# Scaling expert rows by the router weight on their way out of PSUM, and adding them to the residual in memory by an accumulating scatter

## The reference, cut to what matters

```
h = h + mixer_block(rms_norm(h, norm1[l]), ...)
h = h + hier_moe(rms_norm(h, norm2[l]), ...)
return rms_norm(h, norm_f)

# in hier_moe
gates = jnp.sum(jax.nn.one_hot(expert_id, N_EXPERTS, dtype=f32) * top_w[..., None], axis=1)
for e in range(N_EXPERTS):
    h = jax.nn.silu(xt @ w_g[e]) * (xt @ w_u[e])
    out = out + gates[:, e:e + 1] * (h @ w_d[e]).astype(f32)
```

## Time and profile before

| | |
|---|---|
| three runs | 993.78, 997.96, 1000.33 us (median 997.96) |
| the profiled execution | 997.03 us, of which the span that the profile covers is 995.2 us |
| busy over the span | PE 90%, DVE 66%, ACT 49%, POOL 9% |
| memory traffic of the span | 168.30 MB read, 13.07 MB written |
| experts (700 to 940 us) | DMA engines busy throughout |
| mean granted TensorE clock | 0.954 of full speed |

### The profile page before, as it was taken

One profiled execution on the slowest core, in us unless ns is written; L12 is line 12 of the kernel. 1 busy time (PEld: TensorE's weight loads), 2 busy tenths in 40 slices (PEclk: granted clock), 3 DMA queues, 4 the chain that ended last, 5 costly groups with the idle time before them and its releaser, 6 DMA issues.

```text
span 995.2 us, 14556 instructions
## 1 busy us (share of the span) xinstructions
PE 895.0 (90%) x5884; PEld 511.0 (51%) x5884; DVE 657.2 (66%) x864; ACT 490.3 (49%) x684; POOL 91.7 (9%) x90
## 2 busy tenths in 40 slices
PE   5999999999999998999999989518999999989960
PEld 4434784857656564444444489514545444444420
DVE  3677769533886776443444245454899998988926
ACT  5434373324445444323232325614888878778812
POOL 7000000003000000000000000010121122322100
PEclk9999999999999999999999989758999999999985
DMA  8712414437310115933432260283999999999706
GB/s 206 165 31 63 109 35 114 128 86 149 86 32 17 38 38 193 305 94 96 117 100 83 77 213 2 90 314 131 316 394 388 371 365 376 371 369 366 293 24 251
DMA packets 147247, 174.02 MB, mean 175 GB/s; under 512 B 14391, under 2 KB 99695, under 8 KB 147174
## 3 DMA queue, kind: packets, MB, share of 16 engines
q1 hardware_dynamic: 139760, 158.56, 47.7%
q0 software_dynamic: 7136, 13.89, 5.0%
q10 hardware_dynamic: 278, 0.56, 0.2%
HBM read 168.30 MB, written 13.07 MB: 182 GB/s over the span
## 4 chain that ended last, share of the span: by engine, by line
PE 74%; DMA 11%; DVE 10%; ACT 3%; issue 1%; ACTq 0%; POOLq 0%; DVEq 0%; SPq 0%
PE bank L915 20%; PE bank L916 19%; PE bank L917 19%; DMA arena<-in_moe_wu 6%; DMA arena<-in_moe_wg 4%; PE bank L1127 3%; DVE arena L1645 3%; PE bank L1146 3%; ACT arena L800 1%; PE bank L1021 1%; PE bank L1136 1%; PE bank L1284 1%; DMA arena<-x_rows,token_of 1%; PE bank L1218 1%; PE bank L1006 1%
## 5 line engine op out<-in xcount | busy, mean ns | idle before, releaser
L915 PE MATMUL bank<-arena 128*128 128x512 f16 (+1 forms) x1568 | 465.2, 317 | 13.1 <-DVE arena L1392 4.6
L916 PE MATMUL bank<-arena 128*128 128x512 f16 (+1 forms) x1568 | 464.5, 316 | 0.0
L917 PE MATMUL bank<-arena 128*128 128x512 f16 (+1 forms) x1568 | 464.1, 316 | 0.0
L1645 DVE SCALAR_TENSOR_TENSOR arena<-arena 128x2048 f16<-128x2048 f32 x96 | 216.9, 2288 | 50.2 <-ACT arena L800 50.1
L915 PEld LDWEIGHTS bank<-arena 128*128 128x128 f16 x1568 | 155.1, 99 | 141.5 <-issue 33.8
L917 PEld LDWEIGHTS bank<-arena 128*128 128x128 f16 x1568 | 154.9, 99 | 111.3 <-issue 3.2
L916 PEld LDWEIGHTS bank<-arena 128*128 128x128 f16 x1568 | 154.7, 99 | 99.9 <-issue 3.0
L800 ACT ACTIVATE arena<-arena 128x2048 f16<-128x2048 f32 x96 | 181.5, 1909 | 40.1 <-PE bank L1234 12.5
L567 ACT ACTIVATE arena<-arena 128x1024 f16<-128x1024 f32 (+1 forms) x92 | 92.5, 1007 | 101.3 <-PE bank L917 73.5
L1392 DVE SCALAR_TENSOR_TENSOR arena<-arena 128x1024 f16<-128x1024 f32 (+1 forms) x91 | 103.5, 1163 | 11.4 <-ACT arena L567 9.8
L621 ACT ACTIVATE arena<-bank 128x512 f32<-128x512 f32 x35 | 20.8, 595 | 90.8 <-PE bank L917 90.7
(11 more groups left out here) (257 smaller groups left out, 735.9 us busy)
## 6 DMA issues: line engine op xcount, KB each, us to landing
arena<-in_moe_wg SPq DMA_DIRECT2D x32, 1024.0 KB, 16.4
arena<-in_moe_wu SPq DMA_DIRECT2D x32, 1024.0 KB, 16.3
arena<-in_moe_wd SPq DMA_DIRECT2D x32, 1024.0 KB, 15.3
arena<-in_w_gate SPq DMA_DIRECT2D x32, 512.0 KB, 4.1
arena<-in_w_in SPq DMA_DIRECT2D x31, 512.0 KB, 4.3
arena<-in_w_branch SPq DMA_DIRECT2D x32, 192.0 KB, 3.5
arena<-in_w_out SPq DMA_DIRECT2D x8, 512.0 KB, 5.2
arena<-y_rows SPq DMA_DIRECT2D x4, 1024.0 KB, 8.3
```

The source lines that it names most:

```text
L915: pe.matmul(outb, lhs[0], rhs[0], start=first, stop=False, skip_group_check=True)
L916: pe.matmul(outb, lhs[0], rhs[1], start=False, stop=False, skip_group_check=True)
L917: return pe.matmul(outb, lhs[1], rhs[0], start=False, stop=last_, skip_group_check=True)
L1645: tell("split_done", stt(w_lo[c % NW], stage[c % NS], WSCALE, w_hi[c % NW], ALU.mult, ALU.subtract))
```

## The change

Each expert's rows are scaled by the router weight when ACT copies them from PSUM: the scale is now a column `slotw[:, e]`, one number for each slot. The scatter writes them to `h_rows`, which holds one row for each token, with the operation add: the DMA reads the row in memory, adds, and writes it back. `h_rows` (the first 512 rows of the old `y_rows`) is filled with the residual by eight stores behind the `h_done` of each column block. Scatter e now waits for scatter e-1 to have landed, since two experts may add to the same row (before, it waited for e-2). At the end SP loads one row for each token (0.5 MiB for each tile) and DVE adds nothing; in the place of its two operations stands one on a single column, which only passes the signal on. For `slotw`, DVE puts the weights as two float16 halves into `told`, which has a fourth column, and adds them up again after `token_full`. The second-choice mask, `row_of` and the wait of SP for the last split go. After the `Tanh` of the last expert ACT issues a `Sqrt` on one column.

```diff
@@ sync
+            for m in range(KD):
+                sp_.wait_ge(S("h_done"), m + 1)
+                sp_.dma_start(h_rows.rearrange("(t p) n -> p t n", p=P)[:, :, m * P:(m + 1) * P], hres[:, :, m * P:(m + 1) * P]
+                              ).then_inc(S("h_stored"), 16)
             for t in range(NT):
                 sp_.wait_ge(S("x2_ready"), t + 1)
@@
-                sp_.wait_ge(S("split_done"), len(STEPS))
                 for t in range(NT):
-                    sp_.dma_start(yg[t], y_rows.rearrange("(j t p) n -> t p j n", j=2, p=P)[t]
-                                  ).then_inc(S(f"tokens_in{t}"), 16)
+                    sp_.dma_start(hres[:, t, :], h_rows[t * P:(t + 1) * P, :]).then_inc(S(f"tokens_in{t}"), 16)
@@ gpsimd
-                        if e >= 2:
-                            pool.wait_ge(S(f"y_stored{e % 2}"), 16 * (e // 2))
-                        pool.indirect_dma_start(out=y_rows, out_offset=bass.IndirectOffsetOnAxis(ap=row_of[:, e:e + 1], axis=0),
-                                                in_=yout[e % 2], in_offset=None, bounds_check=2 * T - 1, oob_is_err=False
-                                                ).then_inc(S(f"y_stored{e % 2}"), 16)
+                        if e >= 1:
+                            pool.wait_ge(S(f"y_stored{(e - 1) % 2}"), 16 * ((e - 1) // 2 + 1))
+                        else:
+                            pool.wait_ge(S("h_stored"), 16 * KD)
+                        pool.indirect_dma_start(out=h_rows, out_offset=bass.IndirectOffsetOnAxis(ap=token_of[:, e:e + 1], axis=0),
+                                                in_=yout[e % 2], in_offset=None, bounds_check=T - 1, oob_is_err=False,
+                                                compute_op=ALU.add).then_inc(S(f"y_stored{e % 2}"), 16)
@@ scalar
                         act.activation(sgr[e % 2], ps[2 * (e % 2)][:, :], ACT.Tanh, scale=0.5 / WSCALE).then_inc(S("sgr_ready"), 1)
+                        if e == NE - 1:
+                            link(act.activation(stat[:, 2, 0:1], ones[:, 0:1], ACT.Sqrt))
@@
+                        if e == 0:
+                            act.wait_ge(S("slotw_ready"), 1)
                         for j in range(2):
                             act.activation(yout[e % 2][:, 512 * j:512 * (j + 1)], ps[4 + j][:, :], ACT.Copy,
-                                           scale=1.0 / (WSCALE * HSCALE)).then_inc(S("y_out"), 1)
+                                           scale=slotw[:, e:e + 1]).then_inc(S("y_out"), 1)
@@ vector
-            link(dve.tensor_copy(told[:, :, 1, :], selj[:, 1, :, :]))
-            link(dve.memset(told[:, :, 2, :], 1.0))
+            link(dve.memset(told[:, :, 1, :], 1.0))
+            link(tt(selj[:, 0, :, :], selj[:, 0, :, :], w1.to_broadcast([P, NT, NE]), ALU.mult))
+            link(tt(selj[:, 1, :, :], selj[:, 1, :, :], w2.to_broadcast([P, NT, NE]), ALU.mult))
+            link(tt(gates[:, :, :], selj[:, 0, :, :], selj[:, 1, :, :], ALU.add))
+            link(ts(gates[:, :, :], gates[:, :, :], W16, None, ALU.mult))
+            link(dve.tensor_copy(told[:, :, 2, :], gates[:, :, :]))
+            link(tt(told[:, :, 3, :], gates[:, :, :], told[:, :, 2, :], ALU.subtract))
             dve.wait_ge(S("rank_full"), 1)
@@
+            link(dve.tensor_copy(slotv[:, 2, :], got[:, 2, :]))
+            sig("token_read", tt(slotv[:, 2, :], slotv[:, 2, :], got[:, 3, :], ALU.add))
+            sig("slotw_ready", ts(slotw[:, :], slotv[:, 2, :], 1.0 / (WSCALE * HSCALE * W16), None, ALU.mult))
@@
                 def add_rows(t):
                     dve.wait_ge(S(f"tokens_in{t}"), 32)
-                    link(stt(hres[:, t, :], yg[t][:, 0, :], wsel[:, 0, t:t + 1], hres[:, t, :], ALU.mult, ALU.add))
-                    sig("moe_done", stt(hres[:, t, :], yg[t][:, 1, :], wsel[:, 1, t:t + 1], hres[:, t, :], ALU.mult, ALU.add))
+                    sig("moe_done", ts(total[:, 1:2], total[:, 0:1], 1.0, None, ALU.mult))
```

More of the change, by code:

```diff
@@ L46 @@
 HSCALE = 1.0 / 16
+W16 = 1024.0
 AHEAD = 4
@@ L283, in build @@
                 .rearrange("p (k c) -> p k c", c=P) for j in range(2)] for i in range(2)]
-        yg = [view(STAGE[t], 2, D) for t in range(NT)]
         nf = arena[:, 8192:8192 + D]
@@ L330, in build @@
         wsel = sb("wsel", [P, 2, NT])
-        told = ctx.enter_context(nc.sbuf_tensor("told", [P, NT, 3, NE], F16))
+        told = ctx.enter_context(nc.sbuf_tensor("told", [P, NT, 4, NE], F16))
         slotv = sb("slotv", [P, 3, NE])
-        row_of = ctx.enter_context(nc.sbuf_tensor("row_of", [P, NE], U32))
+        slotw = sb("slotw", [P, NE])
         token_of = ctx.enter_context(nc.sbuf_tensor("token_of", [P, NE], U32))
@@ L341, in build @@
         rt_bank = (ps[6], ps[7], ps[2], ps[3])
-        scratch, x2_rows, y_rows = d["bias_scratch"], d["x2_rows"], d["y_rows"]
+        scratch, x2_rows, h_rows = d["bias_scratch"], d["x2_rows"], d["y_rows"][0:T, :]
         MIXW = 20 + 1 + 1
@@ L1233, in _ @@
                 for t in range(NT):
-                    last = pe.matmul(ps[7][:, 3 * e:3 * e + 3], onehot[:, t, :].rearrange("p (c e) -> p e c", e=NE)[:, e, :], told[:, t, :, e],
+                    last = pe.matmul(ps[7][:, 4 * e:4 * e + 4], onehot[:, t, :].rearrange("p (c e) -> p e c", e=NE)[:, e, :], told[:, t, :, e],
                                      start=(t == 0), stop=(t == NT - 1))
@@ L1730, in _ @@
             dve.wait_ge(S("token_full"), 1)
-            got = ps[7][:, 0:3 * NE].rearrange("p (e a) -> p a e", a=3)
-            link(ts(slotv[:, 0, :], got[:, 2, :], -float(NOWHERE), float(NOWHERE), ALU.mult, ALU.add))
+            got = ps[7][:, 0:4 * NE].rearrange("p (e a) -> p a e", a=4)
+            link(ts(slotv[:, 0, :], got[:, 1, :], -float(NOWHERE), float(NOWHERE), ALU.mult, ALU.add))
             link(tt(slotv[:, 1, :], slotv[:, 0, :], got[:, 0, :], ALU.add))
             link(dve.tensor_copy(token_of[:, :], slotv[:, 1, :]))
-            sig("token_read", stt(slotv[:, 2, :], got[:, 1, :], float(T), slotv[:, 1, :], ALU.mult, ALU.add))
-            link(dve.tensor_copy(row_of[:, :], slotv[:, 2, :]))
+            link(dve.tensor_copy(slotv[:, 2, :], got[:, 2, :]))
+            sig("token_read", tt(slotv[:, 2, :], slotv[:, 2, :], got[:, 3, :], ALU.add))
+            sig("slotw_ready", ts(slotw[:, :], slotv[:, 2, :], 1.0 / (WSCALE * HSCALE * W16), None, ALU.mult))
             sig("dense_known", ts(total[:, 1:2], total[:, 0:1], 1.0, None, ALU.mult))
```

## The result

The changed kernel takes 1008.5 us (median of four runs, 1005.94 to 1009.02) against 995.87 us for the kernel before (four runs, 993.55 to 1000.33): a ratio of 1.0117, 95% interval 1.0089 to 1.0145. It is 1.2% slower, a small loss, but the interval leaves no room for equal times. The forecast was 1009, which is 11.8 us above the profiled execution of before; the medians lie 12.6 apart. The profiled execution took 1008.41 us with a span of 1006.6, which is 11.4 above the span before.

What follows compares the result with a forecast made beforehand. The prediction took the DMA engines to bound the expert stage. Its terms, -8.2 + 15.6 + 1.3 + 1.6 + 1.5 = +11.8 us on the profiled 997.03, gave 1008.8, stated as 1009, with a range of 991 to 1016 (0.8).

Steps and rivals of the forecast that it cites:

- The bound: Expert stage, about 700 to 914 us: bound by the DMA engines, so DMA work added there comes out in full.
- The add among the loads: Twelve scatters ahead of the last wait for a load: each add costs a second transfer, 12 x 1.3 = +15.6 us.
- The last scatter: Scatter alone on the chain after the experts: longer by the same price of an add, +1.3 us.
- The end: Final normalisation and stores: smaller loads and no DVE sums, then a circle of 1.9 us per tile; -8.2 us.
- The early root: ACT's Sqrt in the last expert: table load and root stand ahead of the last split, PE waits; +1.6 us.
- Routing: Between masks and first gather: eight DVE operations in place of three, one more before `dense_known`, all on the path; +1.5 us.
- At nothing: Stores of `h`, scatter e's wait for e-1, ACT's scale from a column: claimed to cost nothing.
- A free second read: Rival on scatters: the add's second read runs beside the first or loads don't feel it; 992 us, chance 0.17.
- Felt as a mean: Rival on scatters: less loaded engines take over, 0.65 us per add; 1000 us, chance 0.13.
- Dearer: Rival on scatters: each row read, added and written in turn, three times the plain transfer; 1026 us, chance 0.15.

Runs made afterwards that it cites:

- run 3: The kernel before, with its first twelve scatters issued a second time to a buffer nothing reads, no adding: 1010.61 us, ratio 1.0139.
- run 7: The kernel before with only the table of slot numbers changed, so an expert's slots are dealt out over the partitions: 987.97 us, ratio 0.9909.
- run 1: The changed kernel with all 16 scatters as plain writes in place of adds: 989.59 us, ratio to before 0.9939.
- run 2: The changed kernel with adds in the last four scatters alone, plain writes in the first twelve: 993.91 us, ratio to before 0.9970.
- run 4: The changed kernel with its Sqrt moved out of the experts to the head of the end, ahead of the first square: 1005.43 us, ratio to before 1.0091.
- run 5: The changed kernel without the Sqrt after the last expert's Tanh: 1006.66 us, ratio to before 1.0108.
- run 8: The kernel before with slots dealt out over the partitions and a Sqrt on one column at the head of the end: 986.86 us, ratio 0.9893.

## Why the prediction was right

**The bound.** "The expert stage is bound by the DMA engines": run 3 adds nothing but DMA work there and is 14.2 us slower, run 7 only spreads the same transfers over more DMA engines and is 9 us faster.

**The add among the loads** was put at 12 x 1.3 = 15.6 us. The trace has 13.9, runs 1 and 2 leave 14.6 for it. The step from 18.37 to 19.67 us per expert is the forecast's 19.7. That a row of an add takes twice the engine time is shown by the 98 against 197 GB/s of the scatter alone, and that the price is that of a second transfer by run 3. The count of twelve was read from the trace of before. In the changed kernel the last load that the chain waits for lands at 960.31, behind fourteen scatters (the last of them issued at 956.72), and 14 x 1.3 = 18.2 would be further off. Why the total stays below is not settled, and neither is what the low clock inside the experts (last section) adds to it.
The Trainium skill's rule (Collectives: The Full Stack, The bandwidth ceiling), that in a collective a reduce step runs at half the rate of a copy for its second source read, agrees in size: its 1.93 stands against 2.0 here (98 against 197 GB/s). Which of the two reads holds the engine no run shows.

**The last scatter** was sized too low: +1.3 forecast, +2.7 measured (5.92 against 3.19; 5.98 in run 2, 3.19 in run 1). The doubling of the rows' time is there, but alone in the queues the add also has gaps between rows, 3.5 us for 64 rows. Dealt over all engines it still takes 4.81, where the plain one takes 2.70.

**The end** was put at -8.2 and is -7.6. The two table loads stood where the program's order had them, one in idle time (981.35), one between square and root (994.43).

**The early root**: forecast +1.6, measured 7.0 against 5.4 us, and taken out again in run 4. The drain of 1.38 us that the Trainium skill gives for a switch (ScalarE: Activation LUTs, What ACT_TABLE_LOAD costs) isn't in these rows: the load at 960.33 is followed by the root at 961.62.

**Routing**: forecast +1.5, measured 1.2 up to the ranks and 0.2 behind. I took it as wholly on the path; 0.8 us came back before the third expert's transposes.

**At nothing**: right for the stores of `h` and the new wait (run 1 holds both, and an expert takes 18.3 us there). None of the sixteen scatters was held by the new wait: POOL sat idle before each of them for ACT's copy (121.1 us in all), and an add landed within 11.4 us of its issue. Wrong for ACT's scale from a column: the two copies to `yout` take 1.27 us in place of 1.09.

**The rivals.** A free second read (992) falls with run 1, which shows 18.9 us for the adds. Felt as a mean (1000): the distance of the gathers in run 3 speaks against it. Dearer (1026) holds in part only for the scatter that is alone. The mechanism held, but that the forecast came within 1 us is partly luck, because misses cancel. Against the forecast the trace has 1.7 less for the adds among the loads, 1.4 more for the last scatter, 0.6 more at the end, and 0.9 less for routing. It also has 0.2 for ACT's slower copy, 1.5 us of the mixer and -1.7 of the clock, and the last two go with the two executions and not with the change.

## What to carry to other kernels

An accumulating DMA takes work off DVE at the price of DMA work: here it held its DMA engines twice as long for a row (98 against 197 GB/s), so ask whether the stretch in which it runs is bound by DMA before moving a sum into memory. Look at the busy share of one indirect transfer in a quiet place: here it stood at 0.48 with 197 GB/s, and with the rows dealt over the partitions at 0.98 with 393. That table of constants gave 9 us on the kernel before and 17.6 on the kernel with adds. A warming operation for ACT's table brought nothing ahead of the branch and cost 1.6 us there; behind the branch and in idle time it left one table load where there were three. The program's order tells where the loads fall.

## What the runs showed of the hardware that was not expected

- The profile's bytes don't show the add's read of memory. The queue of the indirect DMAs (packets, MB, share of 16 engines over the span) has the same packets with and without adds, and longer packet times; here the changed kernel, before, and run 3:

```profile
q0 software_dynamic: 7136, 13.90, 6.1%
q0 software_dynamic: 7136, 13.89, 5.0%
q0 software_dynamic: 8864, 16.93, 5.6%
```

  The line of memory traffic can't show it either. In run 3 its written bytes grow by 6.3 MB, which is 12 scatters of all 128 slots of 4 KB, while the queue moved 3.0 MB more: slots that are skipped are counted there. Its 2.1 MB less read in the changed kernel are the shorter end alone.
- PE's clock inside the experts. After PE's waits for loads the granted clock fell to its lower level (1.2 GHz) for 3 to 4 us at a time: in the changed kernel three times (from about 792, 870 and 911 us), in run 3 three times, in runs 4 and 5 twice each, and between 690 and 950 us never in the other six profiles. One of them, in windows of 2 us:

```profile
868.00:870.00 2.00, 0.22 (x2) 0.26 (x3) 1.63 (x2) 1.01 (x1) 0.00 (x0) 1.00 1.01 352
870.00:872.00 2.00, 2.00 (x11) 1.33 (x10) 1.07 (x1) 1.87 (x3) 0.07 (x1) 0.60 1.04 395
872.00:874.00 2.00, 2.00 (x7) 0.70 (x5) 2.00 (x3) 1.41 (x1) 2.00 (x1) 0.55 1.04 394
```

  The DMA engines stay full in it (1.04), so it need not lengthen a stage that waits for loads. These four kernels are those with 19.7 us between gathers, and no run parts the two, so up to 5 us of PE's time (1.7 for each stretch) are a part of the price that isn't separated.
- PE's clock before the last scatter. In the kernel before the granted clock falls to half (1.2 GHz) from about 957.6 to 961, after PE's gap for the last expert's hidden rows, and costs 1.7 us: the last two scatters are issued 9.43 us apart (956.39 and 965.82). In the changed kernel they are 7.93 apart (974.16 and 982.09), with the clock at 1.00 and a gap of the same kind, although ACT's copies take 0.2 longer. Over all ten profiles the distance was 7.7 to 7.9 in four (the changed kernel, runs 5, 7 and 8) and 9.4 to 9.6 in six, with and without the early root. What decides it stays open; it is 1.7 us that a comparison of two single profiles of this kernel can carry either way. A window of before, and one of the changed kernel at the same place in the work:

```profile
958.00:960.00 2.00, 2.00 (x7) 0.63 (x5) 0.00 (x0) 0.00 (x0) 0.00 (x0) 0.50 0.32 123
976.00:978.00 2.00, 2.00 (x11) 0.93 (x10) 0.00 (x0) 0.00 (x0) 0.00 (x0) 1.00 0.60 74
```
